# Feed-forward of a 1024-wide decoder on one core: moving the turned activations by 16 DMA transfers on ScalarE's queue

## What is computed

```python
def swiglu(x, w_gate_up, w_down):
    gate, up = jnp.split(x @ w_gate_up, 2, axis=-1)
    return (jax.nn.silu(gate) * up) @ w_down
...
    ff = swiglu(rms_norm_2(h, g[0]), ffn_w_gate_up[i, 0], ffn_w_down[i, 0])
    h = h + 0.5 * rms_norm_2(ff, g[1])
```

## Time and profile before

| | |
|---|---|
| median of 3 runs | 1418.52 us |
| the profiled execution's own time | 1420.49 us |
| its span, first to last instruction | 1418.7 us |
| TensorE busy | 1396.4 us (98%), clock 0.998 |
| VectorE busy | 1024.2 us (72%) |
| ScalarE busy | 992.2 us (70%) |
| DMA queue of SyncE (q1) | 233.57 MB, 50.3% of 16 engines |
| DMA queue of ScalarE (q10) | 64 packets, 0.02 MB |

### The profile page before, as it was taken

How to read it: one execution, slowest core, us unless ns; L and a number is a source line. 1 busy time by engine, 2 the same in 40 slices (tenths; PEclk the granted TensorE clock), 3 DMA queues, 4 the chain that set the end, 5 groups by cost and what they waited for, 6 DMA issues and landing times.

```text
span 1418.7 us, 20586 instructions
## 1 busy us (share of the span) xinstructions
PE 1396.4 (98%) x7875; PEld 1146.4 (81%) x7875; DVE 1024.2 (72%) x1413; ACT 992.2 (70%) x1762; POOL 69.5 (5%) x163
## 2 busy tenths in 40 slices
PE   7999999999999999999999999999999999999998
PEld 6788888888888887788888888887778888788886
DVE  5878788877666766676667766667989886876665
ACT  6657574747777654577775777867888886577784
POOL 8000000000000000000000000001030300000000
PEclk9999999999999999999999999999999999999999
DMA  7542463345565555466555555646453432566562
GB/s 227 167 144 93 142 203 119 119 137 190 186 200 192 181 188 193 147 206 199 189 197 178 193 192 194 191 169 185 136 164 104 125 123 90 165 206 199 188 205 92
DMA packets 168290, 238.26 MB, mean 168 GB/s; under 512 B 21554, under 2 KB 114640, under 8 KB 168192
## 3 DMA queue, kind: packets, MB, share of 16 engines
q1 hardware_dynamic: 166496, 233.57, 50.3%
q0 software_dynamic: 1632, 3.35, 0.8%
q10 hardware_dynamic: 64, 0.02, 0.0%
HBM read 235.07 MB, written 1.84 MB: 167 GB/s over the span
## 4 chain that ended last, share of the span: by engine, by line
PE 94%; DVE 2%; ACT 2%; DMA 1%; issue 0%; SPq 0%; DVEq 0%; ACTq 0%
PE A L245 18%; PE A L246 17%; PE A L247 17%; PE G L247 5%; PE G L245 5%; PE G L246 5%; PE M L246 5%; PE M L245 5%; PE M L247 5%; PE A L1331 1%; PE G L1252 1%; PE G L1299 1%; DVE tmp L414 1%; PE M L1309 1%; DVE x_lo L419 1%; ACT x_hi L399 1%
## 5 line engine op out<-in xcount | busy, mean ns | idle before, releaser
L227 DVE TENSOR_TENSOR w_lo<-raw,w_hi 128x1024 fp32r<-128x1024 f32 (+2 forms) x296 | 507.0, 1727 | 122.4 <-ACT w_hi L209 121.8
L209 ACT ACTIVATE w_hi<-raw 128x1024 fp32r<-128x1024 f32 (+2 forms) x296 | 427.1, 1462 | 126.4 <-DMA raw<-in_ffn_w_gate_up 97.7
L245 PE MATMUL A<-w_hi,x_hi 128*128 128x512 f32 (+1 forms) x640 | 259.3, 405 | 3.5 <-DVE x_lo L419 1.2
L247 PE MATMUL A<-w_hi,x_lo 128*128 128x512 f32 (+1 forms) x640 | 247.7, 387 | 0.0
L246 PE MATMUL A<-w_lo,x_hi 128*128 128x512 f32 (+1 forms) x640 | 246.9, 386 | 0.0
L690 ACT ACTIVATE ffn_ffn_hT<-ffn_ffn_hb 32x128 f32<-32x128 f32 x512 | 157.1, 307 | 11.7
L245 PEld LDWEIGHTS A<-w_hi,x_hi 128*128 128x128 f32 x640 | 120.7, 189 | 33.4 <-DVE x_lo L419 6.7
L247 PEld LDWEIGHTS A<-w_hi,x_lo 128*128 128x128 f32 x640 | 120.4, 188 | 25.3
L245 PE MATMUL A<-w_hi,ffn_ffn_hT_hi 128*128 128x512 f32 x352 | 139.0, 395 | 0.0
L246 PE MATMUL A<-w_lo,ffn_ffn_hT_hi 128*128 128x512 f32 x352 | 138.3, 393 | 0.0
L246 PEld LDWEIGHTS A<-w_lo,x_hi 128*128 128x128 f32 x640 | 120.9, 189 | 21.2 <-issue 0.7
(11 more groups left out here) (392 smaller groups left out, 2022.3 us busy)
## 6 DMA issues: line engine op xcount, KB each, us to landing
raw<-in_ffn_w_gate_up SPq DMA_DIRECT2D x176, 512.0 KB, 4.7
raw<-in_ffn_w_down SPq DMA_DIRECT2D x88, 512.0 KB, 4.0
raw<-in_w_in SPq DMA_DIRECT2D x48, 512.0 KB, 4.4
raw<-in_gdn_w_in SPq DMA_DIRECT2D x48, 512.0 KB, 4.6
raw<-in_sc_w_in SPq DMA_DIRECT2D x24, 512.0 KB, 4.5
raw<-in_w_out SPq DMA_DIRECT2D x16, 512.0 KB, 4.6
raw<-in_gdn_w_out SPq DMA_DIRECT2D x16, 512.0 KB, 4.3
raw<-in_w_mem_kv SPq DMA_DIRECT2D x8, 512.0 KB, 5.2
```

What stands on the lines that cost most here:

```text
L209: ins = act.activation(net.w_hi[:, v % RING, part], net.raw[:, v % RING, part], ACT.Copy)
L227: ins = dve.tensor_tensor(net.w_lo[:, v % RING, part], net.raw[:, v % RING, part], net.w_hi[:, v % RING, part].bitcast(F32), ALU.subtract)
L245: pe.matmul(out, xh, hi[:, k, c, :], start=start and k == 0, stop=False)
L247: mm = pe.matmul(out, xl, hi[:, k, c, :], start=False, stop=stop and k == nk - 1)
```

## The change

Steps 0 to 8 now go by blocks, so TensorE's transposes of step 0 go. ScalarE's 16 copies of a step become 16 SBUF-to-SBUF transfers issued on ScalarE's own queue, all ahead of the second split; each moves 32 partitions of 512 contiguous bytes, and each adds 16 to `h_moved`, for which `hid_hi` waits. `h`, `hb` and `hT` get other layouts for it, so that VectorE's product writes h in two runs of 128, and `hid_hi` and `hid_lo` read and write in a permuted order. `hid_hi(0)` and `hid_lo(0)` move behind the second split of j = 1, and g(2,0) waits for `hidden` of step 0 instead of its `h_lo`.

```diff
--- before.py
+++ after.py
@@ -561,10 +561,10 @@
         self.clamped = net.shared_sem("ffn_gate", self.steps)
         self.gated = net.shared_sem("ffn_sigmoid", self.steps)
         self.hidden = net.shared_sem("ffn_hidden", self.steps)
-        self.by_blocks = range(1, self.steps - 2)
+        self.by_blocks = range(0, self.steps - 2)
         self.h_turned = net.shared_sem("ffn_h_turned", self.steps - len(self.by_blocks))
         self.h_blocks = net.shared_sem("ffn_h_blocks", len(self.by_blocks))
-        self.h_moved = net.shared_sem("ffn_h_moved", len(self.by_blocks))
+        self.h_moved = net.shared_sem("ffn_h_moved", 256 * len(self.by_blocks))
         self.h_hi = net.shared_sem("ffn_h_hi", self.steps)
         self.h_lo = net.shared_sem("ffn_h_lo", self.steps)
 
@@ -582,9 +582,9 @@
         self.z = net.sb("ffn_z", [P, TT, 256])
         self.e = net.sb("ffn_e", [P, TT, 256])
         self.gs = net.sb("ffn_gs", [P, TT, 256])
-        self.h = net.sb("ffn_h", [P, TT, 256])
-        self.hb = net.sb("ffn_hb", [P, TT, 2, 4, 32])
-        self.hT = net.sb("ffn_hT", [P, 2, TT, 4, 32])
+        self.h = net.sb("ffn_h", [P, 2, TT, P])
+        self.hb = net.sb("ffn_hb", [P, 4, 2, TT, 32])
+        self.hT = net.sb("ffn_hT", [P, 4, 2, TT, 32])
         self.hT_hi = net.sb("ffn_hT_hi", [P, 4, T], F32R)
         self.hT_lo = net.sb("ffn_hT_lo", [P, 4, T], F32R)
 
@@ -614,7 +614,7 @@
 
     def turns(self, j):
 
-        return j + 1 if j == 0 else j + 1 - len(self.by_blocks)
+        return j + 1 - len(self.by_blocks)
 
     def gate_up(self, w, j, kh):
         net = self.net
@@ -632,7 +632,7 @@
         for kk in range(2):
             for tt in range(TT):
                 mm = pe.transpose(bank[:, kk * T + tt * P:kk * T + (tt + 1) * P],
-                                  self.h[:, tt, kk * P:(kk + 1) * P], net.ident[:, :])
+                                  self.h[:, kk, tt, :], net.ident[:, :])
         mm.then_inc(self.h_turned.sem, 1)
 
     def down(self, w, j):
@@ -677,35 +677,31 @@
         w.chain(act.activation(self.e[:, :, :], self.e[:, :, :], ACT.Ln, bias=1.0))
         act.activation(self.e[:, :, :], self.e[:, :, :], ACT.Exp, scale=-1.0).then_inc(self.gated.sem, 1)
 
-    def move(self, w, j, half):
+    def move(self, w, j):
         act = w.eng
         if j not in self.by_blocks:
             return
-        if half == 0:
-            act.wait_ge(*self.h_blocks(j))
-            if j > 1:
-                act.wait_ge(*self.h_lo(j))
-        for i in (2 * half, 2 * half + 1):
+        act.wait_ge(*self.h_blocks(j + 1))
+        if j > 0:
+            act.wait_ge(*self.h_lo(j))
+        for i in range(4):
             for b in range(4):
-                ins = act.activation(self.hT[32 * b:32 * b + 32, :, :, i, :].rearrange("p k t n -> p t k n"),
-                                     self.hb[32 * i:32 * i + 32, :, :, b, :], ACT.Copy)
-                if half == 0 or (i, b) != (3, 3):
-                    w.chain.mark(ins)
-                else:
-                    ins.then_inc(self.h_moved.sem, 1)
+                act.dma_start(self.hT[32 * b:32 * b + 32, i, :, :, :],
+                              self.hb[32 * i:32 * i + 32, b, :, :, :]).then_inc(self.h_moved.sem, 16)
 
     def hid_hi(self, w, j):
         act = w.eng
         at = 2 * (j % 2)
         if j in self.by_blocks:
-            w.chain.sync()
-            act.wait_ge(*self.h_moved(j))
+            act.wait_ge(*self.h_moved(256 * (j + 1)))
             if j >= 2:
                 act.wait_ge(self.net.unit_used, self.unit_end["d", j - 2])
-            src = self.hT[:, :, :, :, :].rearrange("p k t i n -> p (k t i n)")
-        else:
-            act.wait_ge(*self.h_turned(self.turns(j)))
-            src = self.turn_bank(j)[:, :]
+            src = self.hT[:, :, :, :, :].rearrange("p i k t n -> p (k t) i n")
+            act.activation(self.hT_hi[:, at:at + 2, :].rearrange("p k (t i n) -> p (k t) i n", t=TT, i=4), src,
+                           ACT.Copy).then_inc(self.h_hi.sem, 1)
+            return
+        act.wait_ge(*self.h_turned(self.turns(j)))
+        src = self.turn_bank(j)[:, :]
         act.activation(self.hT_hi[:, at:at + 2, :].rearrange("p k t -> p (k t)"), src, ACT.Copy).then_inc(self.h_hi.sem, 1)
 
     def act(self, w):
@@ -720,14 +716,10 @@
         self.sigmoid(w, 0)
         for j in range(1, self.steps):
             w.split_hi()
-            if j == 1:
-                self.hid_hi(w, 0)
-            self.move(w, j - 1, 0)
+            self.move(w, j - 1)
             if j < self.steps - 1:
                 w.split_hi()
-            self.move(w, j - 1, 1)
-            if j > 1:
-                self.hid_hi(w, j - 1)
+            self.hid_hi(w, j - 1)
             self.sigmoid(w, j)
             w.split_hi()
         self.hid_hi(w, self.steps - 1)
@@ -747,26 +739,31 @@
         dve.wait_ge(*self.gated(j + 1))
         w.chain(dve.tensor_tensor(self.gs[:, :, :], self.z[:, :, :], self.e[:, :, :], ALU.mult))
         for tt in range(TT):
-            ins = dve.scalar_tensor_tensor(out=self.h[:, tt, :], in0=self.banks(j)[tt][:, 256:512],
-                                           scalar=net.r[:, tt:tt + 1], in1=self.gs[:, tt, :],
+            ins = dve.scalar_tensor_tensor(out=self.h[:, :, tt, :],
+                                           in0=self.banks(j)[tt][:, 256:512].rearrange("p (k c) -> p k c", k=2),
+                                           scalar=net.r[:, tt:tt + 1],
+                                           in1=self.gs[:, tt, :].rearrange("p (k c) -> p k c", k=2),
                                            op0=ALU.mult, op1=ALU.mult)
         ins.then_inc(self.hidden.sem, 1)
         if j in self.by_blocks:
             dve.wait_ge(*self.hidden(j + 1))
-            if j > 1:
-                dve.wait_ge(*self.h_moved(j - 1))
-            dve.transpose(self.hb[:, :, :, :, :].rearrange("p t k b n -> p (t k b n)"),
-                          self.h[:, :, :].rearrange("p t c -> p (t c)")).then_inc(self.h_blocks.sem, 1)
+            if j > 0:
+                dve.wait_ge(*self.h_moved(256 * j))
+            dve.transpose(self.hb[:, :, :, :, :].rearrange("p b k t n -> p (k t) b n"),
+                          self.h[:, :, :, :].rearrange("p k t (b n) -> p (k t) b n", b=4)).then_inc(self.h_blocks.sem, 1)
 
     def hid_lo(self, w, j):
         dve = w.eng
         dve.wait_ge(*self.h_hi(j + 1))
         at = 2 * (j % 2)
-        src = self.hT[:, :, :, :, :].rearrange("p k t i n -> p (k t i n)") if j in self.by_blocks \
-            else self.turn_bank(j)[:, :]
-        dve.tensor_tensor(self.hT_lo[:, at:at + 2, :].rearrange("p k t -> p (k t)"), src,
-                          self.hT_hi[:, at:at + 2, :].rearrange("p k t -> p (k t)").bitcast(F32),
-                          ALU.subtract).then_inc(self.h_lo.sem, 1)
+        hi, lo = self.hT_hi[:, at:at + 2, :], self.hT_lo[:, at:at + 2, :]
+        if j in self.by_blocks:
+            src = self.hT[:, :, :, :, :].rearrange("p i k t n -> p (k t) i n")
+            hi, lo = (a.rearrange("p k (t i n) -> p (k t) i n", t=TT, i=4) for a in (hi, lo))
+        else:
+            src = self.turn_bank(j)[:, :]
+            hi, lo = (a.rearrange("p k t -> p (k t)") for a in (hi, lo))
+        dve.tensor_tensor(lo, src, hi.bitcast(F32), ALU.subtract).then_inc(self.h_lo.sem, 1)
 
     def dve(self, w):
         dve = w.eng
@@ -783,13 +780,10 @@
         self.gate(w, 0)
         for j in range(1, self.steps):
             w.split_lo()
-            if j == 1:
-                self.hid_lo(w, 0)
             self.clamp(w, j)
             if j < self.steps - 1:
                 w.split_lo()
-            if j > 1:
-                self.hid_lo(w, j - 1)
+            self.hid_lo(w, j - 1)
             self.gate(w, j)
             w.split_lo()
         self.hid_lo(w, self.steps - 1)
```

## The result

The changed kernel takes 1520.01 us in the median, against 1418.78 us for the kernel before: ratio 1.0703, 95% interval 1.0691 to 1.0716. That is 101 us slower, far outside the predicted 1416.8 to 1432.0.

The account below looks back on a forecast made before the run. TensorE, busy for 98% of the span, was taken to bound the kernel; -1.6 us of transposes and +4.7 us of waits gave +3.1 on 1418.5, so 1421.6 us, whole range 1416.8 to 1432.0.

Parts of the forecast that it names:

- the gain on offer: TensorE's four transposes of step 0 go, 0.4 us in each of four feed-forwards: -1.6 us, the whole gain.
- Layouts at 0: VectorE's strided product, transpose and `hid_lo` touch as many elements as before, so the new layouts cost 0.
- copies at 0: ScalarE's 16 copies a step, 4.9 us, lie under TensorE's 16.37 us step, so removing them is worth 0.
- I take 0.49: Pitch of ScalarE's 16 issues a step, from SyncE's run of small transfers: 0.49 us each, 7.84 us a burst.
- I take 2.9: Time from issue to landing of a small transfer on ScalarE's queue: 2.9 us, the median of those seen.
- The chain, "15.2 us": From one step's burst to the next: 15 pitches, landing, `hid_hi`, sigmoid and gate take 15.2 us against TensorE's 16.37.
- An ordinary step ... No stall: In an ordinary step the last transfer lands at 829.5 and `hid_hi` could start 2.1 us earlier; TensorE never waits.
- my rival of the drag: Landing of 4.1 us or pitch of 0.57 makes every step wait: +33 us, 1451, or 1430 if weaker; chance 0.14.
- The start of a feed-forward: Unit 5's split stands behind step 0's burst, so TensorE waits 1.10 to 1.39 us per feed-forward, together +4.7 us.
- None at later units: After the wait at unit 5 of each feed-forward, TensorE waits for no later weight unit; unit 6 is just in time.
- The instructions ahead of a burst need not be over: On ScalarE, issues can start while an earlier instruction runs, so a step's first split may run beside the burst.
- The queues take turns: Rival: SyncE's and ScalarE's issues exclude each other, a burst grows by 1.8 us, 1447.7 us; chance 0.08.

Follow-up runs that it names:

- the first experiment: The changed kernel with its 16 moves a step made by ScalarE copies again, layouts and step 0 by blocks kept: 1418.47 us, ratio 0.9991.
- through HBM: The changed kernel with each step's move made in five issues, one transfer out to HBM and four back, instead of sixteen: 1426.65 us, ratio 1.005.
- the probe: The kernel before, with groups of eight transfers of several kinds added behind its output on ScalarE's and SyncE's queues to measure issue pitch; its time was not compared.
- the interleaved order: The changed kernel with eight of a step's 16 issues ahead of the second split and eight behind it: 1516.74 us, ratio 1.0685.
- the two-queue kernel: The changed kernel with eight of a step's 16 transfers on ScalarE's queue and eight on SyncE's, between weight loads: 1463.03 us, ratio 1.0305.

## Why the prediction was wrong, step by step

**What bounds the kernel, and the gain on offer: right.** TensorE bounded it; the only gain was in its transposes. Without those of step 0 the first experiment is 1.3 us below before (ratio 0.9991), and without those of step 9 as well 3.7 us (0.9974); I had 1.6 us for step 0's in the prediction, and the same for step 9's ahead of its run; the intervals hold that.

**Layouts at 0: right; copies at 0: nothing speaks against it.** The kernel with the new layouts and copies is at 0.9991. ScalarE's busy time fell by 158 us in the changed kernel and by as much through HBM, and neither is faster than the one with copies; no run takes the copies away and puts nothing in their place.

**"I take 0.49, because only that row shows a long run": the step that failed.** The pitch was 0.64, outside my ends of 0.42 and 0.53. All the rows that I bounded it by were transfers from HBM to SBUF; the probe gives 0.46 to 0.47 for such and 0.63 to 0.64 for SBUF to SBUF. I had written that no row showed the kind asked for, and then let nearby rows of another kind be the ends of the range. An end above them should have come from the price at which the answer changes, 0.57, which stood in the text.

**"I take 2.9" for the landing: mis-sized, too.** The median was 3.0, but the chain needs the last of a burst: 5.0 us in the second burst, for the burst from 362.52 some 4.6 (last issue about 372.0, `hid_hi` at 376.60), and 4.3 in the median of all. The argument that ScalarE's queue carries no loads did not protect it: alone the transfers took 1.8 us, beside the weight loads up to 5.4. That the loads delay them is what these two numbers suggest; no run varied the loads by themselves.

**The chain, "15.2 us": the form was right, the terms were not.** 15 x 0.64 + 4.6 + 0.54 + 4.32 + 0.1 = 19.2 us; 19.0 was measured. "So the chain keeps up, with 1.2 us to spare" was false, and with it "An ordinary step ... No stall". This was my rival of the drag, at a chance of 0.14: its condition (pitch over 0.57, or landing over 4.1) held twice over, and it was priced for a late landing alone, +33 us. With both it is 2.6 to 2.8 us a step. Nine steps in each of four feed-forwards, as that rival counts them, would make 94 to 101 us; that this meets the measured loss is in part luck, since nine bursts have only eight distances between them, and the clamps put 77.5 us into the steps and 23.5 into the starts. The knee between 8 and 16 transfers, the interleaved order that changed next to nothing, and eight steps costing 71 us show this mechanism rather than argue it.

**The start of a feed-forward: right in place, short in size.** The first wait came at unit 5, 3.79 us against 1.11; with the measured pitch my sum gives 1.11 + 16 x 0.15 = 3.5. The four together are 15.7 us against 4.7. "None at later units" was wrong: 49 waits followed.

**The instructions ahead of a burst need not be over: right** (342.39 inside the split from 341.68).

**The queues take turns: fell as priced.** In the changed kernel 170 of the 576 issues ran beside one of SyncE's, and their median of 0.61 us is that of the other 406. In the probe, with both queues issuing at once, each kept its pitch but for one issue. Where both issued such transfers beside the weight loads, in the two-queue kernel, 48 of ScalarE's 288 issues took over 0.7 us, against 19 of 576 in the changed one; what stretched them is not shown. The rule of the Trainium skill, Perfetto Trace Analysis, section DMA Instruction — HWDGE (DVE, Sync), that the block which generates descriptors is locked for exclusive use, shows in the probe in no more than that one issue of 0.83 us.

**Not in the prediction at all: the clock.** Waits of TensorE were priced at their length. Of the 96 us up to 13 are matmuls at 1.2 GHz behind the waits, and about as much is the 0.3 us of busy time that each wait adds.

## What to carry to other kernels

A DMA issue is an instruction in the program of the engine that issues it, and it holds up that engine's next instructions: here 0.64 us each, twice the 0.31 us copy it replaced. Count issues before bytes, and compare the burst plus its last landing with the slack of the loop that waits for it; under the slack it is nearly free (8 of them cost 0.2%), above it every iteration pays (16 cost 7%). Where no row shows the price of an operation, set the range by the price at which the answer would turn, not by the nearest rows of another kind.

## What the runs showed of the hardware that I had not expected

- A transfer from SBUF to SBUF costs 0.63 to 0.64 us of pitch on either queue, from HBM to SBUF 0.46 to 0.47, and 128 partitions cost within 0.01 us of 32.
- Beside weight loads `hid_hi` got its data 3.0 to 5.4 us after the last of 16 small transfers was issued, 4.3 in the median; such a transfer landed 1.8 us after its issue in the median without them.
- After a wait of 3.79 us TensorE's matmuls of 512 columns came every 0.43 us instead of 0.23 for some 3 us, with a granted clock of 0.51. Within the span the clock stood at 1.2 GHz for 56.7 us in the interleaved kernel, with 33 waits of up to 4.4 us, and for 4.0 us in the one with transfers for steps 1 to 8, with 51 waits of at most 2.1 us.
